# Choosing 256 tokens for each of 16 experts: sorted extraction by eights replaced by a search for the cut-off value

## What is computed

```python
def expert_choice_ffn(h, w_router, w_gate, w_up, w_down):
    cap = EC_CAPACITY_FACTOR * t_ // N_EXPERTS            # 256
    aff = jax.nn.softmax(jnp.einsum('btd,de->bte', h, w_router).astype(jnp.float32), axis=-1)
    top_aff, top_idx = lax.top_k(jnp.swapaxes(aff, 1, 2), cap)
    xe = h[bidx, top_idx]
    hid = jax.nn.silu(jnp.einsum('becd,edf->becf', xe, w_gate)) * jnp.einsum('becd,edf->becf', xe, w_up)
    ye = jnp.einsum('becf,efd->becd', hid, w_down) * top_aff[..., None]
    return jnp.zeros_like(h).at[bidx, top_idx].add(ye)
```

## Time and profile before

| | us |
|---|---|
| median of 3 runs | 4271.92 (4267.68 to 4272.87) |
| the profiled execution, device time | 4263.5 |
| its span, first to last instruction | 4261.9 |
| TensorE busy in the span | 3982.3 (93%) |
| VectorE busy | 2371.7 (56%) |
| ScalarE busy | 1525.9 (36%) |
| GpSimd busy | 778.6 (18%) |
| mean granted TensorE clock, share of full speed | 0.969 |

### The profile page before, as it was taken

One profiled execution on the slowest core, in us unless ns is written; L12 is line 12 of the kernel. 1 busy time (PEld: TensorE's weight loads), 2 busy tenths in 40 slices (PEclk: granted clock), 3 DMA queues, 4 the chain that ended last, 5 costly groups with the idle time before them and its releaser, 6 DMA issues. The chain is left out here.

```text
span 4261.9 us, 57779 instructions
## 1 busy us (share of the span) xinstructions
PE 3982.3 (93%) x20052; PEld 3060.1 (72%) x20052; DVE 2371.7 (56%) x3119; ACT 1525.9 (36%) x2467; POOL 778.6 (18%) x698
## 2 busy tenths in 40 slices
PE   8999999999989999998999999999159999999998
PEld 3444446456769999998778778788048888888887
DVE  5555420355646666665443534354876777777675
ACT  5333311225642222222342424222124444444443
POOL 3877100011113333332000000000100010101000
PEclk9999999999999999999999999999579999999999
DMA  7234241011132222221535434243137676767673
GB/s 302 88 109 121 62 127 34 16 54 39 25 136 64 74 78 84 74 74 42 199 103 173 158 106 156 80 157 141 74 128 217 215 215 211 214 210 215 203 217 103
DMA packets 234601, 542.97 MB, mean 127 GB/s; under 512 B 35164, under 2 KB 95868, under 8 KB 231804
## 3 DMA queue, kind: packets, MB, share of 16 engines
q1 hardware_dynamic: 202380, 426.69, 31.2%
q0 software_dynamic: 32112, 114.84, 9.1%
HBM read 439.95 MB, written 99.55 MB: 127 GB/s over the span
## 5 line engine op out<-in xcount | busy, mean ns | idle before, releaser
L2693 DVE TENSOR_TENSOR sb_we_low<-sb_we,sb_we_high 128x1024 fp32r<-128x1024 f32 x377 | 458.3, 1223 | 127.3 <-ACT sb_we_high L2645 127.3
L2645 ACT ACTIVATE sb_we_high<-sb_we 128x1024 fp32r<-128x1024 f32 x377 | 392.2, 1048 | 147.8 <-PE ey L2609 147.8
L307 PE MATMUL p_ps<-sb_hT,sb_ring 128*128 128x512 f32 (+1 forms) x960 | 379.5, 553 | 1.8 <-ACT sb_raw L450 1.8
L2114 DVE TENSOR_TENSOR sb_wm_low<-sb_wm,sb_wm_high 128x1024 fp32r<-128x1024 f32 x127 | 155.3, 1224 | 398.7 <-ACT sb_wm_high L2027 398.7
L2594 PE MATMUL eg<-sb_xe_parts,sb_we_high 128*128 128x512 f32 x1024 | 370.9, 395 | 1.6 <-DVE sb_xe_parts L2688 1.6
L2594 PE MATMUL eu<-sb_xe_parts,sb_we_high 128*128 128x512 f32 x1024 | 370.9, 394 | 0.0
L307 PEld LDWEIGHTS p_ps<-sb_hT,sb_ring 128*128 128x128 f32 x960 | 184.0, 192 | 189.1 <-issue 180.9
L1969 PE MATMUL pg<-sb_hb_high,sb_wm_high 128*128 128x512 f32 x768 | 303.3, 395 | 9.4 <-DVEq L2086 5.3
L1971 PE MATMUL pg<-sb_hb_high,sb_wm_low 128*128 128x512 f32 x768 | 300.3, 391 | 0.0
L1970 PE MATMUL pg<-sb_hb_low,sb_wm_high 128*128 128x512 f32 x768 | 300.1, 391 | 0.0
L2593 PE MATMUL eu<-sb_xe_parts,sb_we_low 128*128 128x256 f32 x896 | 251.7, 281 | 0.0
(11 more groups left out here) (411 smaller groups left out, 8547.7 us busy)
## 6 DMA issues: line engine op xcount, KB each, us to landing
sb_we<-in_w_ex SPq DMA_DIRECT2D x384, 512.0 KB, 4.4
sb_wm<-in_w_gates SPq DMA_DIRECT2D x96, 512.0 KB, 3.6
sb_wrow<-in_w_mod_row POOLq DMA_DIRECT2D x64, 256.0 KB, 3.5
sb_wm<-in_w_br SPq DMA_DIRECT2D x32, 512.0 KB, 4.5
sb_ring<-in_w_ch POOLq DMA_DIRECT2D x19, 512.0 KB, 3.8
sb_eg<-eg_d SPq DMA_DIRECT2D x36, 256.0 KB, 4.1
sb_lk<-k_d SPq DMA_DIRECT2D x36, 256.0 KB, 4.5
sb_lq<-q_d SPq DMA_DIRECT2D x36, 256.0 KB, 4.8
```

The costliest lines, as they stand in the source:

```text
L307: last = nc.tensor.matmul(ps[:, b % BANKS, 0:wd], w[:, kind, k], g.hT[:, k, t0:t0 + wd], start=(k == 0), stop=(k == KD - 1))
L2114: v.tensor_tensor(wl[n], w[n], wh[n], ALU.subtract).then_inc(s.wl, 1)
L2645: nc.scalar.activation(wh[:, n % CUT], w[:, n % RAW], ACT.Copy).then_inc(s.wh, 1)
L2693: v.tensor_tensor(wl[:, n % CUT], w[:, n % RAW], wh[:, n % CUT], ALU.subtract).then_inc(s.wl, 1)
```

## The change

`choose` no longer extracts. `experts` takes the weights from elsewhere. In words:

- **Layout.** The affinities are transposed by two transposes into `aff`, 128 partitions x 256: partition 16 j + e holds tokens of expert e. A table `ctab` (128 x 501 floats, some 256 KB) is loaded ahead of everything else on SyncE.
- **Search.** The 256th largest affinity of each expert is found as a bit pattern, two bits a round. A round: three candidates (base OR'd with three steps); three TENSOR_SCALARs over `aff` that compare with a candidate and count into one column each; a product on TensorE that adds the counts of an expert's 8 partitions; a TENSOR_SCALAR that counts how many candidates still have 256 at or above them; two small operations that put the two bits into the base. 15 rounds.
- **Places.** One compare for "above", one for "equal", a running sum to break ties, a second running sum to number the chosen tokens, with small products between for offsets across partitions.
- **Lists.** Two transposes, place split into high and low 4 bits, eight TENSOR_TENSORs of 128 x 1024 that compare them with 0..15, 16 ScalarE activations that scale by the token number, 32 products of 128 x 128 x 128 that add the tokens into place, then a few small steps to `top_idx`.
- **Weights.** `h2_d` gets 16 more columns: SyncE stores the affinities there in two DMAs, 2048 pieces of 64 bytes, after its weight loads, and waits for them inside `choose`. The gather fetches 1040 floats a row, not 1024, and `low_rows` copies the weight column from the gathered rows; `pick` copies the token numbers alone.

```diff
             @blk.sync
+                sp.dma_start(tab[:], g.ctab).then_inc(s.tab, 16)
                 sp.dma_start(g.gt2, g.rows_d[:, 3]).then_inc(g.ew.gt, 16)
                 for n in range(RAW):
                     sp.dma_start(g.we[:, n], g.w_ex[0, n]).then_inc(g.ew[n], 16)
+                sp.wait_ge(s.aff, 2)
+                for h in range(2):
+                    sp.dma_start(g.h2_d[:, D:D + E].rearrange("(j h p) e -> p h j e", h=2, p=P)[:, h],
+                                 lg2[:, h].rearrange("p (j e) -> p j e", e=E)).then_inc(s.st, 16)
+                sp.wait_ge(s.st, 32)
...
             @blk.scalar
+                for q, (h, j0) in enumerate(QS):
+                    act.wait_ge(s.lo, q + 1)
+                    for j in range(j0, j0 + HT // 2):
+                        nc.scalar.activation(named[:, h, j]..., at_lo[:, h, j * E:(j + 1) * E]...,
+                                             ACT.Copy, scale=toks[:, 2 * j + h:2 * j + h + 1]).then_inc(s.wt, 1)
             @blk.tensor
+                for i in range(ROUNDS):
+                    pe.wait_ge(s.acc, LV * (i + 1))
+                    nc.tensor.matmul(pc[:, 0:LV], same_e, tall[:, 0:LV], start=True, stop=True).then_inc(s.cnt, 1)
...
+                for q, (h, j0) in enumerate(QS):
+                    pe.wait_ge(s.hi, q + 1)
+                    for j in range(j0, j0 + HT // 2):
+                        pe.wait_ge(s.wt, HT * h + j + 1)
+                        for u in range(2):
+                            last = nc.tensor.matmul(po[u][:, 0:P], at_hi[:, h, j * E + u * HE:j * E + (u + 1) * HE]...,
+                                                    named[:, h, j, u], ...)
             @blk.vector
-                for r in range(CAP // 8):
-                    at = slice(8 * r, 8 * r + 8)
-                    own.done(v.max(val[:, at], aff[:]))
-                    own.settle()
-                    v.max_index(idx[:, at], val[:, at], aff[:]).then_inc(s.mi, 1)
-                    own.done(v.match_replace(aff[:], val[:, at], aff[:], -1.0))
+                for i in range(ROUNDS):
+                    own.done(v.tensor_tensor(cand[:], steps[:, i], base[:].broadcast_to([P, LV]), ALU.bitwise_or))
                     own.settle()
+                    for n in range(LV):
+                        v.tensor_scalar((more, same, run)[n][:], aff[:], levels[:, n:n + 1], 0.0, ALU.is_ge, ALU.add, accum_out=tall[:, n:n + 1]).then_inc(s.acc, 1)
+                    dve.wait_ge(s.cnt, i + 1)
+                    own.done(v.tensor_scalar(held[:], pc[:, 0:LV], float(CAP), 0.0, ALU.is_ge, ALU.add, accum_out=passed[:]))
+                    own.settle()
+                    own.done(v.tensor_scalar(gain[:], passed[:], float(1 << (2 * (ROUNDS - 1 - i))), None, ALU.mult))
+                    own.settle()
+                    own.done(v.tensor_tensor(base[:], base[:], gain[:], ALU.bitwise_or))
+                    own.settle()
+                v.tensor_scalar(more[:], aff[:], level, 0.0, ALU.is_gt, ALU.add, accum_out=tall[:, LV + 0:LV + 1]).then_inc(s.tally, 1)
+                v.tensor_scalar(same[:], aff[:], level, 0.0, ALU.is_equal, ALU.add, accum_out=tall[:, LV + 1:LV + 2]).then_inc(s.tally, 1)
+                dve.wait_ge(s.tally, 2)
+                own.done(v.tensor_tensor_scan(run[:], same[:], same[:], 0.0, ALU.add, ALU.max))
+                dve.wait_ge(s.lim, 1)
+                own.done(v.tensor_scalar(lim[:, 0:1], pl[:, 0:1], -1.0, float(CAP), ALU.mult, ALU.add))
+                own.settle()
+                own.done(v.scalar_tensor_tensor(same[:], run[:], lim[:, 0:1], same[:], ALU.is_le, ALU.mult))
+                own.settle()
+                v.scalar_tensor_tensor(more[:], same[:], 1.0, more[:], ALU.mult, ALU.add, accum_out=tall[:, LV + 2:LV + 3]).then_inc(s.sum, 1)
+                dve.wait_ge(s.sum, 1)
+                own.done(v.tensor_tensor_scan(run[:], more[:], more[:], 0.0, ALU.add, ALU.max))
+                dve.wait_ge(s.off, 1)
+                own.done(v.tensor_copy(lim[:, 1:2], pl[:, 1:2]))
+                own.settle()
+                v.scalar_tensor_tensor(run[:], run[:], lim[:, 1:2], more[:], ALU.add, ALU.mult).then_inc(s.slot, 1)
...
+                for h, j0 in QS:
+                    at = slice(j0 * E, (j0 + HT // 2) * E)
+                    n = HT // 2 * E
+                    v.tensor_tensor(at_lo[:, h, at], lo[:, h, at][:, :, None].broadcast_to([P, n, SUB]),
+                                    los[:, None, :].broadcast_to([P, n, SUB]), ALU.is_equal).then_inc(s.lo, 1)
+                    v.tensor_tensor(at_hi[:, h, at], hi[:, h, at][:, :, None].broadcast_to([P, n, SUB]),
+                                    his[:, None, :].broadcast_to([P, n, SUB]), ALU.is_equal).then_inc(s.hi, 1)
+                dve.wait_ge(s.pick, 1)
...
 def experts(nc, g):
-        xe = sbuf(nc, c, "xe", [P, HALF, D])
+        xe = sbuf(nc, c, "xe", [P, HALF, D + E])
...
                 def gather(e, u):
-                    pool.wait_ge(s.pick, 2 * e + 2)
+                    pool.wait_ge(s.pick, e + 1)
+                    wait(pool, s.weight, e)
                     wait(pool, s.tr, 4 * e)
...
                 def low_rows(e, u):
+                    dve.wait_ge(s_ga[u], 32 * ((e - u) // 2) + 32 if isinstance(e, int) else e * 16 + (2 - u) * 16)
+                    v.tensor_copy(ta[:, u], xe[:, :, bass.ds(at + D, 1)].rearrange("p a e -> p (a e)")).then_inc(s.weight, 1)
```

More of the change, by code:

```diff
@@ L69 @@
 F_W = F_K2 + 2 * P
+K_SAME, K_PRE, K_BLK = 0, P, 2 * P
+K_FOLD = 3 * P
+K_SPR = K_FOLD + E // 2
+K_HI = K_SPR + 16
+K_LO = K_HI + 16
+K_TOK = K_LO + 16
+K_STEP = K_TOK + LT
+K_W = K_STEP + 45
 class Steps:
@@ L2396, in choose @@
[L2396 to L2403, removed]
+        aff = sbuf(nc, c, "aff", [P, 2 * P])
+        more, same, run = (sbuf(nc, c, n, [P, 2 * P]) for n in ("c_more", "c_same", "c_run"))
@@ new lines, in choose @@
+        base, gain = (sbuf(nc, c, n, [P, 1], I32) for n in ("c_base", "c_gain"))
+        cand = sbuf(nc, c, "c_cand", [P, LV], I32)
+        steps = sbuf(nc, c, "c_steps", [P, ROUNDS, LV], I32)
+        passed = sbuf(nc, c, "c_passed", [P, 1])
+        held = sbuf(nc, c, "c_held", [P, LV])
+        tall = sbuf(nc, c, "c_tall", [P, LV + 3])
+        lim = sbuf(nc, c, "c_lim", [P, 2])
+        slot, lo, hi = (sbuf(nc, c, n, [P, 2, P], I32) for n in ("c_slot", "c_lo", "c_hi"))
+        at_hi, at_lo = (sbuf(nc, c, n, [P, 2, P, SUB]) for n in ("c_at_hi", "c_at_lo"))
@@ new lines, in choose @@
+        named = sbuf(nc, c, "c_named", [P, 2, HT, 2, P])
+        kept = sbuf(nc, c, "c_kept", [P, 2, P])
+        part = sbuf(nc, c, "c_part", [P, 2, SUB])
+        wide = sbuf(nc, c, "c_wide", [P, 2, HE, SUB])
+        QS = [(h, j) for h in range(2) for j in (0, HT // 2)]
+        ps = psum(nc, c, "aff_ps")
+        pc = psum(nc, c, "cnt_ps")
+        pl = psum(nc, c, "lim_ps")
+        pt = psum(nc, c, "slot_ps")
+        po = [psum(nc, c, f"pick_ps{n}") for n in range(2)]
+        pf = psum(nc, c, "end_ps")
@@ L2404, in _ @@
+        same_e, earlier, block, fold, spread, his, los, toks = (
+            tab[:, at:at + n] for at, n in ((K_SAME, P), (K_PRE, P), (K_BLK, P), (K_FOLD, HE), (K_SPR, SUB), (K_HI, SUB), (K_LO, SUB), (K_TOK, LT)))
+        s = sems(nc, c, "ch", "tab high own ex aff tr trc acc cnt cut tally lim sum off slot turned lohi hi lo st wt pick keep wide end mg")
+        with nc.Block() as blk:
+            @blk.sync
             def _(sp):
+                sp.dma_start(tab[:], g.ctab).then_inc(s.tab, 16)
@@ L2456, in _ @@
                 own.settle()
[L2457 to L2465 removed]
+                for h in range(2):
+                    v.tensor_tensor(lg2[:, h].rearrange("p (j e) -> p j e", e=E), lg.rearrange("p (j h) e -> p h j e", h=2)[:, h],
+                                    over.rearrange("p (j h) e -> p h j e", h=2)[:, h], ALU.mult).then_inc(s.aff, 1)
@@ new lines, in _ @@
+                dve.wait_ge(s.pick, 1)
+                for u in range(2):
+                    v.tensor_tensor(kept[:, u], po[u][:, 0:P], block, ALU.mult).then_inc(s.keep, 1)
+                dve.wait_ge(s.keep, 2)
+                own = Steps(dve, s.mg)
+                own.done(v.tensor_reduce(part[:], kept[:].rearrange("p u (e l) -> p u l e", l=SUB), AX_X, ALU.add))
+                own.settle()
+                v.tensor_tensor(wide[:], part[:][:, :, None, :].broadcast_to([P, 2, HE, SUB]),
+                                fold[:, None, :, None].broadcast_to([P, 2, HE, SUB]), ALU.mult).then_inc(s.wide, 1)
@@ L2493, in _ @@
+                dve.wait_ge(s.end, 1)
+                for u in range(2):
+                    own.done(v.tensor_copy(g.top_idx[:, :, u * HE:(u + 1) * HE], pf[:, u * SUB:(u + 1) * SUB].rearrange("p (a e) -> p a e", a=NS)))
                 own.settle()
```

127 lines of the change are left out of this document (68 added, 59 removed).

## The result

| | us |
|---|---|
| before, median of 4 runs | 4272.40 (4267.68 to 4274.79) |
| changed kernel, median of 4 runs | 4218.75 (4218.29 to 4220.03) |
| ratio | 0.9876, 95% interval 0.9859 to 0.9893 |
| predicted | 4223.2, range 4208 to 4239 |
| span of the profiled execution, before and after | 4261.9 and 4216.7 |

The account below looks back on a forecast made before the run. The prediction took a serial VectorE chain of 127.2 us to bound the stage; terms 1.1 + 46.7 + 7.8 + 6.5 + 13.7 + 2.7 = 78.5 gave a 48.7 us gain, so 4223.2 us, range 4208 to 4239.

Parts of the forecast that it names:

- What bounds the stage: From softmax to top_idx: one serial chain on VectorE, 127.2 us before; shortening it shortens the kernel one for one.
- One round: One round of the search in choose: 3.11 us, so 15 rounds take 46.7 us.
- Two elements a cycle for the compares?: Search compares: the faster float32 rate would save some 0.13 us each, 6 us in all; forecast kept one element a cycle.
- Collisions: Early search rounds: small VectorE operations with two SBUF inputs wait for GpSimd's whole operation in flight, costing 7.8 us.
- Rival 1: Early search: small operations slip between GpSimd's, no collisions; 7.8 us less, 4215 us; chance 0.17.
- Rival 2: Search: reading each compare's sum costs 0.19 us and TensorE's trip 0.97, a round 3.86; total 4235 us; chance 0.15.
- Places, the end, getting to the search: Numbering chosen tokens 6.5 us, final steps to top_idx 2.7, transposes and copy before the search 1.1.
- Lists: Building the token lists after the places: 13.7 us, limited by TensorE, whose clock rises after 3.5 us of unbroken work.
- Rival 3: Lists: TensorE's clock does not rise because its work there has gaps; 7.8 us more, 4231 us; chance 0.10.
- Stores and gathers cost nothing: Affinity stores done by 3040 us, chain ends at 3081; wider gathers have 9.5 us of cover, only the first bare, 0.1 us.
- "TensorE unbroken from the first expert on": Experts' stage: a sign that TensorE runs without waits there; a wait for a gather beyond the first would be wrong.
- The number: Whole kernel: 4214.8 us for the profiled execution, plus 8.4 for the median of runs, giving 4223.2 us.

Follow-up runs that it names:

- both edits: Changed kernel with c_base in PSUM, ratio to before 0.9876; changed kernel with GpSimd's seven low-part operations each cut into four, ratio 0.9874.
- e7_gap_before: Kernel before plus an unused tile of 32 floats per partition behind xe, shifting later buffers 128 bytes; ratio to before 0.9991.
- e5_pad_after: Changed kernel plus 17 small unused TensorE products ahead of choose's transposes, 256 added instructions against before; ratio to before 0.9870.
- 444: Changed kernel with c_base in PSUM and 64 small unused TensorE products, 444 instructions more than before ahead of the experts' loop; ratio to before 0.9854.
- 220: Changed kernel with c_base in PSUM and 8 small unused TensorE products before the lists, 220 instructions more than before; 4230.97 us, ratio to before 0.9909.
- e4_pad_before: Kernel before plus 47 small unused TensorE products in choose, 188 added instructions, as many as the change adds; ratio to before 1.0005.
- 188: The changed kernel's count of TensorE instructions added ahead of the experts' loop against the kernel before; ratio to before 0.9876.
- e12_after_again: Changed kernel run again unedited, as the control; 4214.86 us, ratio to before 0.9869.
- e11_best: Changed kernel with c_base in PSUM, three small unused TensorE products per round and four 128 columns wide before the lists; 4198.75 us, ratio to before 0.9832.
- e8_half: Changed kernel with c_base in PSUM, three small unused TensorE products per round and four before the lists, 384 added instructions; ratio to before 0.9841.

## Why the prediction was right, and where it was off

- **What bounds the stage**, one serial chain on VectorE that shortens the kernel one for one: right. 7 rounds less gave 19.05 of 19.25 us.
- **One round**, 3.11 against 2.75: the largest miss of the sum, 5.4 us. Two sizes were off. I took 0.07 for the read of each compare's sum; it costs nothing, since it runs beside the next compare. From the first compare to the read-out of TensorE's counts it takes 1.97 us (3031.41 to 3033.38), where 1.44 + 0.10 + 0.70 = 2.24 stood. And the read-out costs 0.20, not 0.27. TensorE's 0.70 was right (0.68), the small steps too (0.20).
- **Two elements a cycle for the compares?** The prediction kept one, against the rule of the Trainium skill (VectorE: DVE Perf Modes, The perf-mode tier table). The compares' 0.48 us bears that out, and its page SBUF — State Buffer (Who interferes with whom), which excepts the form with an accumulator. The plain TENSOR_SCALARs of the same size in SBUF, `c_hi` and `c_lo`, took 0.29 and start 0.21 apart, so a faster rate exists in this kernel. They differ from the compares in more than the accumulator (int32 values, and constants in place of a candidate per partition), so no run here shows which of these costs the compares the rate.
- **Collisions**, 7.8 against 8.5: right in mechanism (shown by both edits) and size, though two rounds took nearly all of it, 4.2 us each, not three with 1.7, 4.0 and 2.2. GpSimd started 4.6 us after the softmax, where 4.3 was forecast. Rival 1 is out. Rival 2, dear rounds, is out too, and its sum does not add up: 15 x 0.75 = 11.3 us for the rounds and 11 - 7.8 = 3.2 for their collisions make 14.5, not 11.6, so 4238, not 4235; the range's end at 4239 holds either way.
- **Places, the end, getting to the search**: each within 0.25 us. The running sum of 256 elements, for which there was no row, took 0.69, not 0.6.
- **Lists**, 13.7 against 12.18: the clock rises, as forecast, but some 4.9 us after TensorE's first product where 3.5 stood. What made up for it is the price of a product: 21 records in 2 us at the high clock are 0.19 us for a product of two, not the 0.28 of the earlier trace rows, and 11 in 2 us at the low one 0.36, not 0.6. In the other executions the lists took 11.3 to 12.8. Rival 3 is out.
- **Stores and gathers cost nothing**: right. The stores were issued at 3011.81 and landed 14.5 us later in the median, and TensorE had no wait for a gather after the first; they land at 5.9 us in the median and 9.4 at most, 5.7 and 9.2 before.
- **"TensorE unbroken from the first expert on"**: wrong. The step that failed is the one that costed the experts' stage by its gathers and copies alone. It got 3.8 us shorter by addresses (`e7_gap_before`) and 8.9 longer by the place of its code (`e5_pad_after`), together the 5.0 that the two traces differ by. The sum had no term for either.
- **The number.** Against the profiled execution, device time 4218.29, I was 3.5 us low: 6.4 too much in the stretch, 4.9 of scatter ahead of it and 5.0 in the experts' stage the other way. I then added 8.4 us because the profiled execution of before lay that far under its median; that of after lay 0.5 under its own. So 4223.2 came out 4.5 above. The errors offset each other, and the nearness of the number proves less than the terms do.

## What to carry to other kernels

Where a serial chain meets another engine's long operations, look at the small steps of the chain for two inputs in SBUF: moving one to PSUM took 8.5 us off the search, at 0.01 us an operation. After any edit that adds instructions ahead of a long loop, compare the step per pass and the instruction queue's packets with those of the kernel before; a few unused instructions in idle time took away 9 us here, and a bad number of them added 34. Measure such effects in the profile, by one stage, since the median's interval of 0.17% here hides anything below 7 us.

## Not expected of the hardware

- **The loop's fetch depends on its place.** TensorE's loop over pairs of experts runs nearly without fetching when it lies well (3 packets between its third and its last transposes in `e5_pad_after`) and fetches in every pass when it doesn't (57 in the changed kernel, with 444 and with 220, 9 in nearly every pass; 9 a pass in `e4_pad_before` too, up to its last). The Trainium skill gives 64 bytes for an instruction of VectorE (DVE: opcode table, instruction layouts, handler registers and perf-mode slots, From opcode to uOp program). The packets are 1.08 MB / 66 = 16.4 KB. If TensorE's instructions have the same size, one packet is an estimated 256 instructions, which no run here shows by itself. Good and bad placements repeat with 256 as far as tried: 0 with 256, and 188 with 444. One reading, not tested, is that the engine keeps a fixed number of such blocks and that a loop which touches one more drops what it will need next. The number of packets doesn't give the price: 57 cost 9 us at 188 and 34 us at 220, and 51 cost 3 us in `e4_pad_before`, so it also matters what TensorE executes when the block is missing.
- **Addresses change a product's time by 2%.** 0.233 or 0.229 us for 512 columns in the down projection, by 128 bytes of shift in the buffers behind `xe` (`e7_gap_before`).
- **When TensorE's clock rises scatters.** In the changed kernel and `e12_after_again`, one code, the granted clock left 0.50 some 4 and 11 us after the first expert's transposes began; the step to the second expert took 39.13 and 41.83 us, which is most of the 3.0 us between their X. In the lists it rose 3 to 6 us after the first product, over all kernels. In `e11_best` it rose only after 3086, with the first expert's transposes at 3075.40, where in `e8_half` it rose within 4 us of them. That is what X of 1130.8 against 1128.2 consists of.
